# The order of two pieces of work on ScalarE in the attention slots of a two-layer hybrid transformer kernel

## The reference, cut to what matters

```python
s_loc = jnp.where(band, s_loc, NEG_INF)
p_loc, p_ctx = _joint_softmax(s_loc, s_ctx, s_sink)
o = (jnp.einsum('bhgnqk,bnkhd->bnqhgd', p_loc.astype(v.dtype), vw)
     + jnp.einsum('bhgnqk,bkhd->bnqhgd', p_ctx.astype(v.dtype), vc))
```

## Time and profile before

| | |
|---|---|
| median of 3 runs | 3334.58 us (3331.59 to 3334.59) |
| the profiled execution | 3334.39 us |
| its span | 3332.6 us |
| TensorE matmul busy | 2858.8 us (86%) |
| VectorE busy | 1392.0 us (42%) |
| ScalarE busy | 886.1 us (27%) |
| GpSimd busy | 557.6 us (17%) |

### The profile page before, as it was taken

One profiled execution on the slowest core, in us unless ns is written; L12 is line 12 of the kernel. 1 busy time (PEld: TensorE's weight loads), 2 busy tenths in 40 slices (PEclk: granted clock), 3 DMA queues, 4 the chain that ended last, 5 costly groups with the idle time before them and its releaser, 6 DMA issues. The chain is left out here.

```text
span 3332.6 us, 40345 instructions
## 1 busy us (share of the span) xinstructions
PE 2858.8 (86%) x15572; PEld 2328.3 (70%) x15572; DVE 1392.0 (42%) x2191; ACT 886.1 (27%) x1664; POOL 557.6 (17%) x377
## 2 busy tenths in 40 slices
PE   3477776869799999999994799999877999999993
PEld 0166665748588888888883688888665888888882
DVE  1156563136433333333338355555554333333336
ACT  0133333324312121212113344334333221122111
POOL 0000000113312121212126100000013222221124
PEclk8778788979899999999996899999988999999997
DMA  9721002034201010101013211110053111111114
GB/s 366 284 81 29 21 21 72 19 120 133 85 29 47 29 48 27 49 27 49 27 38 114 81 45 39 33 45 20 7 171 101 51 50 50 50 44 44 50 38 114
DMA packets 201373, 228.92 MB, mean 69 GB/s; under 512 B 15000, under 2 KB 148720, under 8 KB 201264
## 3 DMA queue, kind: packets, MB, share of 16 engines
q1 hardware_dynamic: 200800, 227.19, 21.8%
q10 hardware_dynamic: 464, 0.23, 0.0%
HBM read 198.98 MB, written 32.63 MB: 70 GB/s over the span
## 5 line engine op out<-in xcount | busy, mean ns | idle before, releaser
L1434 PE MATMUL pair<-hth,m_wah 128*128 128x512 f32 (+1 forms) x1280 | 480.1, 375 | 27.8 <-POOL m_wal L1346 27.8
L1368 DVE TENSOR_TENSOR y<-y,pair 128x1024 f32<-128x1024 f32 x288 | 351.2, 1220 | 337.4 <-PE pair L1420 337.2
L1435 PE MATMUL pair<-htl,m_wah 128*128 128x512 f32 (+1 forms) x1280 | 480.0, 375 | 0.0
L1436 PE MATMUL pair<-hth,m_wal 128*128 128x512 f32 (+1 forms) x1280 | 479.5, 375 | 0.0
L1418 PE MATMUL pair<-m_wbh,m_ath 128*128 128x512 f32 x1152 | 449.2, 390 | 4.6 <-DVE y L1368 4.6
L1420 PE MATMUL pair<-m_wbh,m_atl 128*128 128x512 f32 x1152 | 449.5, 390 | 0.0
L1419 PE MATMUL pair<-m_wbl,m_ath 128*128 128x512 f32 x1152 | 449.4, 390 | 0.0
L1396 DVE TENSOR_TENSOR m_atl<-m_sq,m_ath 128x512 fp32r<-128x512 f32 x160 | 102.2, 639 | 715.5 <-POOL m_sq L1353 715.5
L1336 ACT ACTIVATE m_rel<-pair 128x512 f32<-128x512 f32 x160 | 88.7, 554 | 1037.2 <-PE pair L1436 1037.2
L1353 POOL TENSOR_TENSOR m_sq<-m_rel 128x512 f32<-128x512 f32 x160 | 154.5, 965 | 1231.3 <-ACT m_rel L1336 1231.3
L1434 PEld LDWEIGHTS pair<-hth,m_wah 128*128 128x128 f32 x1280 | 242.4, 189 | 76.1 <-POOL m_wal L1346 28.6
(11 more groups left out here) (171 smaller groups left out, 4460.6 us busy)
## 6 DMA issues: line engine op xcount, KB each, us to landing
mod_w<-in_w_mod SPq DMA_DIRECT2D x24, 2048.0 KB, 20.0
m_rawa<-in_mlp_w SPq DMA_DIRECT2D x64, 512.0 KB, 4.2
m_rawb<-in_mlp_w SPq DMA_DIRECT2D x64, 512.0 KB, 4.2
x_rows<-r_res SPq DMA_DIRECT2D x28, 512.0 KB, 3.1
r_raw<-cat_cols SPq DMA_DIRECT2D x18, 512.0 KB, 5.9
m_rawa<-x_rows SPq DMA_DIRECT2D x18, 512.0 KB, 3.8
r_xin<-in_x SPq DMA_DIRECT2D x16, 512.0 KB, 3.9
skewed_rpb<-padded_rpb SPq DMA_DIRECT2D x8, 512.0 KB, 6.4
```

The source lines that it names most:

```text
L1368: dve.tensor_tensor(k.y[:, t, :], k.y[:, t, :], k.pair[t % 2][:, :], ALU.add).then_inc(s_y, 1)
L1434: pe.matmul(o, wah[:, m, kt, :], xh, start=kt == 0, stop=False)
L1435: pe.matmul(o, wah[:, m, kt, :], xl, start=False, stop=False)
L1436: i = pe.matmul(o, wal[:, m, kt, :], xh, start=False, stop=kt == KT - 1)
```

## The change

In a slot n that has no projection and no turned values, ScalarE's list has the copy of unit n-1's transposes ahead of unit n's exponentials. In the other slots the order stays. No instruction is added or removed, and no other engine's list changes.

```diff
             for n in range(N + 1):
+                late = n in at_step or n in turn_step
+                if n and not late:
+                    evacuate(n - 1)
                 if n < N:
                     exps(n)
-                if n:
+                if n and late:
                     evacuate(n - 1)
                 if n in at_step:
                     high(at_step[n])
```

## The result

The changed kernel takes 3305.68 us (median of 4, 3301.38 to 3307.0) against 3334.59 us of the kernel before: a ratio of 0.9911, 95% interval 0.9899 to 0.9924, so 29 us faster. The forecast of order, 19 us, was right, and about 10 us more came from TensorE's clock.

What follows compares the result with a forecast made beforehand. It took each attention slot to be bounded by TensorE's products waiting for ScalarE's copy. Seven kinds of changed slot, 38 in all, summed to 19.0 us: 3334.5 - 19.0 = 3315.5 us, eight in ten within 3307 to 3324.

Steps and rivals of the forecast that it cites:

- The forecast of order, 19 us: Both attention stages: ScalarE's earlier copy lets TensorE's products start sooner, 19.0 us in all, with no change of clock.
- What bounds a slot, and what is late next: Attention slots: products wait for ScalarE's copy, ending 0.57 us after DVE's last; then for DVE's last copy plus 0.15 us.
- The count and the sum, 19.0 us: 38 changed slots, 30 in layer 0 and eight in layer 1, gain 14.7 and 4.3 us.
- the terms: Seven kinds of changed slot, by tiles copied and unit width, each gaining 0.24 to 0.80 us.
- The cost of the move, nothing: Changed slots: exponentials start 0.29 us later, covered by idle time; taken as nothing, at most 11.0 us.
- the forecast with a clock about as before: Whole kernel: TensorE's granted clock stays about the same, so the time is 3312 to 3319 us; chance 0.66.
- Rival 1: Attention slots: TensorE's clock moves too; four fewer low slots give 3309.5 us (chance 0.17), four more 3321.5 (0.10).
- a lean: Attention slots: by the skill's rule on activity, denser slots tend to more full clock; no size of its own.
- Rival 3: Every changed slot: the copy holds exponentials, scaling and DVE's next maxima, 0.29 us x 38 = 11.0 us, 3345.5; chance 0.03.
- the slower side: Whole kernel: the outcome that the change makes it slower than before; chance 0.03.

Runs made afterwards that it cites:

- dve_more: Changed kernel with one more 256-column copy on VectorE ahead of its own copies in layer 0's slots without a projection: 3311.19 us, ratio 0.9937.
- fill: Kernel before, old order, with eight identity transposes on TensorE between its transposes and products in slots without a projection: 3309.41 us, ratio 0.9938.
- all_early: Changed kernel with ScalarE's copy ahead of the exponentials in every slot, those with a projection too: 3302.47 us, ratio 0.9905.
- l0_only: Kernel before with the new order in layer 0 alone: 3314.28 us, ratio 0.9945.
- l1_only: Kernel before with the new order in layer 1 alone: 3324.27 us, ratio 0.9973.

## Why the prediction was wrong

- **What bounds a slot, and what is late next**: right. The releaser changed from ACT to DVE, 0.15 us after its last copy, and "dve_more" moved the slot by the pitch of a copy.
- **The count and the sum, 19.0 us**: right in all that can be separated. A full-clock slot lost 0.48. From the first exponential to slot 30's products layer 0 went from 223.8 to 209.4 us; the terms give 10.4 of these 14.4. From there to the stage's last products it went from 49.6 to 43.1, 6.5, of which the terms give 4.2. Layer 1 lost 8.3, of which they give 4.4 (the terms add up to 14.6 and 4.4, not to the 14.7 and 4.3 that the prediction gives for the layers).
- **The cost of the move, nothing**: right; DVE's second reciprocal keeps its place, and DVE's copies their 0.69 and 0.41 us beside ScalarE's reading.
- **The failed step is "the forecast with a clock about as before", at 0.66.** The three remainders, 4.0 + 2.3 + 4.0, make the 10 us. Rival 1's faster side was the case that came (0.17), and it was priced too low: four slots of 1.5 us, 3309.5. Eight slots with such a stretch behind short waits lost it: slots 32 and 35 in layer 0's end, 60, 61 and 63 in layer 1's, and 7, 17 and 27. Against the same slots at full clock they had cost 2.1, 4.1 and 4.3 us, 10.6 in all. The argument against rival 1, that the low stretches in the mixed part follow the long waits of the projection slots, was right for most of them, which stayed, and overlooked the three that followed a wait of 1.94 us. I held that 0.93 and 0.90 neither showed nor excluded a lean. But the clock fell there, and no wait in those slots was longer than 2.2 us: such waits were enough, and the change takes a quarter of exactly those.
- The Trainium skill ("TensorE: Matmul & The Clock Gate", Part 1) says that TensorE's activity releases its clock from half rate. I left it out of the sum; "fill", which adds nothing but activity, agrees with it: 21 us.
- **Rival 3 and the slower side**: the strict order on ScalarE did hold the exponentials, by 0.2 us here (0.29 forecast) and by more in "all_early", and even there it cost 0.55 us a slot at most.

## What to carry to other kernels

When a change shortens a wait of TensorE inside a loop whose granted clock is under 1, count the low slots in the timeline and price the case that all of them go; a few fillings in that wait, in the old order, show by themselves what the clock can give (4.0 us in layer 1, as much as the change got there, and 17.9 in layer 0, where the change got 6.3). What a reordering gives is the distance to the second-latest releaser, its latency read from a slot where it is the last; that one is the next to shorten. Before fearing that something is held by a reordering, look whether the engine behind it is held by the same event anyway.

## What the runs showed of the hardware

Idle work can pay: 8 useless transposes a slot gave 21 us, 24 of them in each of six places about 12 us over the changed kernel (ratios 0.9876 and 0.9915). With 1.8 to 2.2 us of idle time ahead of the products, in slots of about 5 to 5.6 us, TensorE fell to 1.2 GHz in two to four of the last eight to ten slots of a stage, in all four such stretches (before, "l0_only", "l1_only"); with 1.46 us in 5.10 in none, in seven traces. A low stretch of a few microseconds cost a slot 0.8 to 1.6 us.
